# Expert choice with held weight columns, and a state-space entry normalised by feature columns

## The reference, cut to what matters

```python
# first layer, second half (x: 256 x 2048)
moe = _hier_moe(x, w_rg, b_rg, w_re, b_re, w_gate, w_up, w_down)   # logits: x @ (2048 x 36) + bias
ple = sigmoid(x @ w_pg) * (p @ w_ple)
x   = _layer_norm(ALPHA * x + moe + ple, ln2_w, ln2_b)   # (x - mean) * rsqrt(var + 1e-5) * w + b
# even layer, its entry
h = x * rsqrt(mean(x * x) + 1e-6) * norm_even_g_2        # root-mean-square norm
u, q, k, v, z = split(h @ w_in_even_2)
# state space: per state, decay magnitude exp(lr*dt) and angle li*dt; x_t = lambda x_(t-1) + B u_t; y = C x + D u
x = x + concat(attention, gated state space) @ w_out_even_2
```

## Time and profile before

| | |
|---|---|
| three runs | 3125.07, 3126.21, 3127.43 us; median 3126.21 |
| profiled execution, its own time | 3128.54 us, of which the span is 3126.8 us |
| busy share of the span | TensorE 94%, VectorE 50%, ScalarE 27%, GpSimd 7% |
| chain that ended last | TensorE 62%, VectorE 19%, DMA 12%, ScalarE 4%, issue 1%, GpSimd 1% |
| expert choice, experts | about 985 to 1081 us, 1081 to 2042 us |
| entry of the even layer, its state space loop | 2042 to 2131 us, 2131 to 2346 us |
| the rest of the even layer, the odd layer | to 2660 us, to the end |

### The profile page before, as it was taken

How to read it: one execution, slowest core, us unless ns; L and a number is a source line. 1 busy time by engine, 2 the same in 40 slices (tenths; PEclk the granted TensorE clock), 3 DMA queues, 4 the chain that set the end, 5 groups by cost and what they waited for, 6 DMA issues and landing times.

```text
span 3126.8 us, 42398 instructions
## 1 busy us (share of the span) xinstructions
PE 2943.7 (94%) x18154; PEld 2098.8 (67%) x18154; DVE 1552.9 (50%) x1879; ACT 837.6 (27%) x926; POOL 231.1 (7%) x239
## 2 busy tenths in 40 slices
PE   8999999999999999999999999879999998999898
PEld 6778777999887733333333333267758888998886
DVE  5675544574556513223222222257997554444755
ACT  4532223444433311011011110110001333444443
POOL 2001110000000000000000000035540000100100
PEclk9999998999998999999999999989999999999999
DMA  7653321455564699999999999844444465888553
GB/s 239 192 166 91 94 77 60 130 169 177 189 222 147 223 414 425 425 425 425 425 425 425 425 425 426 361 150 129 138 131 128 135 179 124 201 190 184 128 169 135
DMA packets 218362, 728.66 MB, mean 233 GB/s; under 512 B 16755, under 2 KB 19489, under 8 KB 167863
## 3 DMA queue, kind: packets, MB, share of 16 engines
q1 hardware_dynamic: 212935, 705.65, 64.4%
q0 software_dynamic: 4144, 18.14, 1.7%
q10 hardware_dynamic: 1088, 2.10, 0.2%
HBM read 720.28 MB, written 2.11 MB: 231 GB/s over the span
## 4 chain that ended last, share of the span: by engine, by line
PE 62%; DVE 19%; DMA 12%; ACT 4%; issue 1%; POOL 1%; DVEq 0%; SPq 0%; ACTq 0%
PE psum L137 60%; DVE t L287 13%; DMA t<-in_w_up 12%; ACT t L258 3%; DVE t L298 2%; DVE t L306 1%; POOL t L332 1%; PE psum L143 1%; DVE t L273 1%; ACT t L260 1%; DVE t L302 1%; DMA t<-t 0%; DVE t L310 0%; ACT L258 0%; ACT L260 0%
## 5 line engine op out<-in xcount | busy, mean ns | idle before, releaser
L137 PE MATMUL psum<-t,t 128*128 128x256 f32 (+10 forms) x17124 | 2857.9, 378 | 130.6 <-DVE t L287 77.7
L137 PEld LDWEIGHTS psum<-t,t 128*128 128x128 f32 (+6 forms) x17124 | 2016.2, 174 | 932.8 <-issue 555.4
L287 DVE TENSOR_TENSOR t<-t,t 128x1024 fp32r<-128x1024 f32 (+6 forms) x686 | 822.2, 1199 | 494.8 <-ACT t L258 449.3
L258 ACT ACTIVATE t<-t 128x1024 fp32r<-128x1024 f32 (+7 forms) x523 | 530.7, 1015 | 861.8 <-PE psum L137 572.6
L287 DVE TENSOR_TENSOR t<-t,psum 128x1024 f32<-128x1024 f32 (+3 forms) x258 | 238.2, 923 | 742.4 <-PE psum L137 446.0
L258 ACT ACTIVATE t<-psum 128x1024 f32<-128x1024 f32 (+4 forms) x278 | 213.8, 769 | 1385.4 <-PE psum L137 1280.7
L332 POOL TENSOR_TENSOR t<-t,t 128x1024 f32<-128x1024 f32 (+8 forms) x117 | 174.9, 1495 | 569.4 <-DVE t L287 423.0
L287 DVE TENSOR_TENSOR t<-psum,t 128x1024 f32<-128x1024 f32 (+6 forms) x117 | 101.1, 864 | 116.3 <-PE psum L137 85.9
L143 PE MATMUL psum<-t,t 128*128 128x128 f32 (+1 forms) x518 | 81.2, 292 | 32.0 <-DVE t L298 18.2
L143 PEld LDWEIGHTS psum<-t,t 128*128 128x128 f32 (+1 forms) x518 | 60.2, 147 | 71.2 <-issue 40.9
L83 POOL DMA_DIRECT2D t<-in_s_lr x1 | 0.6, 574 | 1185.0 <-DVE t L310 1185.0
(11 more groups left out here) (66 smaller groups left out, 219.8 us busy)
## 6 DMA issues: line engine op xcount, KB each, us to landing
t<-in_w_gate SPq DMA_DIRECT2D x128, 1024.0 KB, 16.9
t<-in_w_up SPq DMA_DIRECT2D x128, 1024.0 KB, 18.4
t<-in_w_down SPq DMA_DIRECT2D x128, 1024.0 KB, 17.4
t<-in_w_in SPq DMA_DIRECT2D x160, 512.0 KB, 3.6
t<-in_w_in_odd SPq DMA_DIRECT2D x128, 512.0 KB, 5.6
t<-in_w_in_even SPq DMA_DIRECT2D x96, 512.0 KB, 3.8
t<-in_w_out SPq DMA_DIRECT2D x32, 512.0 KB, 4.6
t<-in_w_pg SPq DMA_DIRECT2D x32, 512.0 KB, 4.6
```

The lines of the kernel that those rows point to most:

```text
L137: ins = self.e.matmul(o, l, r, start=start, stop=stop, skip_group_check=True)
L258: self.put(self.e.activation(o, i, f, scale=scale), event)
L287: self.put(self.e.tensor_tensor(o, a, b, op), event)
```

## The change

It has two parts, and some that follow from them.

**Expert choice.** `logits_of` keeps the 36 routing columns as weights and moves all 256 tokens past them: 48 matmuls give 36 x 256 logits. ScalarE copies them out of PSUM, and `route` turns them back with two matmuls against the identity, behind the second piece of `pl.g1`. The copies and subtractions for `xm` are cut in four and put in front of the four quarters of the gate projection.

The diff, cut to its core:

```diff
+def logits_of(of):
+    ps = pe.take("mo.logits", of=of)
+    pe.wait_ge(("mo.wr",))
+    for k in range(16):
+        pe.mm(ps[0:36, 0:256], wrh[:, k, :], x1T[0][:, k, :], k == 0, False)
+        pe.mm(ps[0:36, 0:256], wrh[:, k, :], x1T[1][:, k, :], False, False)
+        pe.mm(ps[0:36, 0:256], wrl[:, k, :], x1T[0][:, k, :], False, k == 15,
+              event=("mo.logits",) if k == 15 else None)
 def route(of):
     ps = pe.take("mo.route", of=of)
-    pe.wait_ge(("mo.wr",), ("landed.route",))
+    pe.wait_ge(("mo.turned",), ("landed.route",))
     for b in range(2):
         o = ps[:, 512 * b:512 * b + 36]
-        tb = slice(128 * b, 128 * b + 128)
         pe.mm(o, ones[0:1, 0:128], br[0:1, :], True, False)
-        for k in range(16):
-            pe.mm(o, x1T[0][:, k, tb], wrh[:, k, :], False, False)
-            pe.mm(o, x1T[1][:, k, tb], wrh[:, k, :], False, False)
-            pe.mm(o, x1T[0][:, k, tb], wrl[:, k, :], False, k == 15,
-                  event=("mo.route",) if b == 1 and k == 15 else None)
+        pe.mm(o, turned_logits[0:36, 128 * b:128 * b + 128], ident[0:36, 0:36], False, True,
+              event=("mo.route",) if b else None)
...
 def even():
     first = native_b("ev.u", hTe, "w_in_even_2", 3072, 1024, (1, 2))
-    for k in range(8):
-        pe.wait_ge(("ev.hT", 2 * k + 1))
-        some(first, 1)
+    def turned_pairs(j):
+        w = pe.take("ev.T", j, of=(0, 3)).rearrange("p (k b t) -> p k b t", b=2, k=4)
+        pe.wait_ge(("l2.x", j), j > 1 and ("ev.hTs", j - 2) or None)
...
+    turned_pairs(0)
+    for j in range(4):
+        if j < 3:
+            turned_pairs(j + 1)
+        for i in (2 * j, 2 * j + 1):
+            pe.wait_ge(("ev.hT", 2 * i + 1))
+            some(first, 1)
+    ps = pe.take("r1.sum", of=(0, 3))
+    pe.wait_ge(("r1.squares",), ("ev.hTs", 3))
+    pe.mm(ps[:, 0:256], ones[:, 0:128], squares[0][:, 0, :], True, True, event=("r1.sum",))
     some(first, 8)
-    rest = chain(native_b("ev.q", hTe, "w_in_even_2", 0, 1024, (0, 1)),
+    def queries():
+        work = native_b("ev.q", hTe, "w_in_even_2", 0, 1024, (0, 1))
+        for i in range(16):
+            if i < 8:
+                pe.wait_ge(("ev.hTn", i // 2))
+            yield next(work)
+    rest = chain(queries(),
                  native_b("ev.k", hTe, "w_in_even_2", 1024, 1024, (0, 1)),
                  native_a("ev.v", hTe, "w_in_even_2", 2048, 1024, (0, 1)),
...
+logits_of(other)
...
-    some(gates, 4)
+    gates = pieces_a(pe, f"pl.g{c}", x1T, 16, "w_pg", 512 * c, 512, of=other if c == 2 else first_of)
+    some(gates, 2)
+    if c == 1:
+        route(other)
+    some(gates, 2)
     if c == 2:
         rank()
     if c == 3:
...
-total = pe.take("r1.sum", of=(0,))
-for j in range(5):
-    if j < 4:
-        turn_columns("ev.T", x, j, ("l2.x", j), of=(1, 2, 3))
-    if j:
-        pe.wait_ge(("r1.square", j - 1))
-        for k in range(4):
...
+    v.wait_ge(("l2.std",))
     v.rcp(inv, stdev)
-    for ci in range(4):
-        cs = slice(512 * ci, 512 * ci + 512)
+    def centred(j):
         for b in range(2):
-            xc = x[:, b, cs]
-            v.stt(xc, xc, mv[:, b, 0:1], l2w[:, cs], ALU.subtract, ALU.mult)
-            v.stt(xc, xc, inv[:, b:b + 1], l2b[:, cs], ALU.mult, ALU.add, event=("l2.x", ci) if b else None)
...
+    def gained(j):
+        ps = v.bank("ev.T", j).rearrange("p (k b t) -> p k b t", b=2, k=4)
+        v.wait_ge(("ev.T", j))
+        for k in range(4):
+            i = 4 * j + k
+            if k == 2:
+                v.wait_ge(("r1.square", j, 1))
+            v.ts(hTe[:, i, :].rearrange("p (b t) -> p b t", b=2), ps[:, k], l2g[:, 0, i:i + 1],
+                 l2g[:, 1, i:i + 1], ALU.mult, ALU.add, event=("ev.hT", i))
+        v.names(("ev.hTs", j))
+    centred(0)
...
+    def squared(j):
+        v.wait_ge(("r1.square", 0, 0), ("r1.square", j, 0))
+        v.tt(squares[0], squares[0], squares[j], ALU.add)
...
+    gained(0)
+    centred(2)
+    gained(1)
+    centred(3)
+    gained(2)
+    squared(1)
+    gained(3)
+    squared(2)
+    squared(3)
+    s0 = squares[0]
+    v.tt(s0[:, 0:2], s0[:, 0:2], s0[:, 2:4], ALU.add)
+    v.tt(s0[:, 0], s0[:, 0], s0[:, 1], ALU.add, event=("r1.squares",))
...
+def states_in(ci):
+    v.wait_ge(("ev.u", ci))
+    v.tt(uT[:, 4 * ci:4 * ci + 4, :], v.bank("ev.u", ci).rearrange("p (m t) -> p m t", m=4), over_tokens(4),
+         ALU.mult, event=("ev.u.c", ci))
+    v.free("ev.u", ci)
+def scaled_tokens(g4):
+    v.wait_ge(("used", "s", stream.turn + 9 + 2 * g4))
+    h4 = hTe[:, 4 * g4:4 * g4 + 4, :]
+    v.tt(h4, h4, over_tokens(4), ALU.mult, event=("ev.hTn", g4))
...
+    v.split_to(first + 13)
+def low_part(c):
+    v.wait_ge(("mo.xmh", c))
+    v.tt(token_part(xm[1], c), token_part(x, c, True), token_part(xm[0], c).bitcast(F32), ALU.subtract,
+         event=("mo.xm", c))
...
     for ex in range(34):
...
+        if 8 <= ex < 11:
+            (s5_decay, s5_angles, s5_factors)[ex - 8]()
         if ex < 32:
             weighted(ex)
         if ex > 1:
...
 def even():
     s5_setup()
+    token_scales()
+    states_in(0)
+    for g4 in range(4):
+        scaled_tokens(g4)
+    states_in(1)
...
     softmax_norm("ev", 2, scs[0], mxs[0])
     softmax_norm("ev", 3, scs[1], mxs[1])
     v.limit = 1 << 20
-    v.wait_ge(("s5.phases", 7))
+    v.wait_ge(("l2.rest", 1))
...
+def s5_decay():
     v.wait_ge(("s5.dt",))
...
+def s5_factors():
     v.wait_ge(("s5.cos",))
...
+    v.tt(ci_, tA, den, ALU.mult, event=("s5.factors",))
+def s5_setup():
+    v.wait_ge(("landed.s5",))
...
-    xp = x.rearrange("p b (q j) -> p b j q", j=16)
-    for b in range(2):
-        a.copy(xm[0][:, b, :].rearrange("p (j q) -> p j q", j=16), xp[:, b], event=("mo.xmh", b))
-        a.split_to(first + 11 + 3 * b)
+    ps = a.bank("mo.logits")
+    a.split_to(first + 11)
+    a.wait_ge(("mo.logits",))
+    a.copy(turned_logits[0:36, :], ps[0:36, 0:256], event=("mo.turned",))
+    a.free("mo.logits")
...
         gathered(0, kq)
     a.wait_ge(("pl.mul", 3))
     for ex in range(33):
+        if ex == 8:
+            a.wait_ge(("landed.s5a",))
+            a.activation(dt, ld, ACT.Exp, event=("s5.dt",))
+        elif ex == 9:
+            a.wait_ge(("s5.lrdt",))
+            a.activation(mag, mag, ACT.Exp, event=("s5.mag",))
+        elif ex == 10:
+            a.wait_ge(("s5.angles",))
+            a.activation(sn, sn, ACT.Sin)
...
-    a.wait_ge(("ev.scored", 3), ("s5.phases", 7))
+    a.wait_ge(("ev.scored", 3), ("l2.rest", 1))
...
+    a.copy(token_part(xm[0], c), token_part(x, c, True), event=("mo.xmh", c))
...
-    ps = a.bank("ev.T", j).rearrange("p (b k t) -> p b k t", b=2, k=4)
...
+    a.wait_ge(("ev.T", j))
+    for k in (2, 3, 0, 1):
+        i = 4 * j + k
+        if k == 0:
+            a.wait_ge(("ev.hT", i + 1))
+        a.activation(squares[j][:, k, :].rearrange("p (b t) -> p b t", b=2), ps[:, k], ACT.Square,
+                     bias=l2c[:, 1, i:i + 1], scale=l2c[:, 0, i:i + 1], event=("r1.square", j, k // 2))
     a.free("ev.T", j)
...
-g.wait_ge(("mo.flagged",))
+g.wait_ge(("mo.flagged",), ("pl.mul", 3))
+g.load(("landed.s5a",), [(lr, I["s5_lr"]), (li, I["s5_li"]),
...
-g.wait_ge(("s5.setup",))
+g.wait_ge(("s5.factors",))
...
+g.wait_ge(("s5.setup",))
 make_phases(0)
 make_phases(1)
 for j in range(6):
     make_phases(j + 2, ("s5.phased", j))
+g.wait_ge(("s5.phases", 7))
+for h in range(2):
+    ch = slice(1024 * h, 1024 * h + 1024)
+    g.load(("landed.l2", h), [(l2w, along("ln2_w")[:, ch]), (l2b, along("ln2_b")[:, ch])])
+    g.wait_ge(("landed.l2", h))
+    for b in range(2):
+        g.tt(x[:, b, ch], x[:, b, ch], l2w, ALU.mult)
+        g.tt(x[:, b, ch], x[:, b, ch], l2b, ALU.add, event=("l2.rest", h) if b else None)
+    g.wait_ge(("l2.rest", h))
...
     quarter(i)
+s.wait_ge(("mo.gu", 27))
+pieces(stream, stream.turn, stream.turn + 4)
+s.wait_ge(("mo.gu", 31))
+pieces(stream, stream.turn + 4, stream.turn + 6)
```

More of the change, by code:

```diff
@@ L166, in __init__ @@
         self.raw, self.hi, self.lo = bufs
+        self.raw = [self.raw[(k - turn) % len(self.raw)] for k in range(len(self.raw))]
         self.known = known
@@ L498, in build @@
         gu = alloc(512)
-        xg = [alloc(4096).rearrange("p (j s) -> p j s", j=16) for _ in range(2)]
         assert top[0] == 12288
@@ L506, in build @@
         place = {key: i for i, key in enumerate(loads)}
-        loads += [("ln2_w", 0, 0), ("ln2_b", 0, 0)]
-        l2w, l2b = [slots[(len(loads) - 2 + k) % 10] for k in range(2)]
         top[0] = free_from
@@ L541, in build @@
         scratch = at(bre_at, 1024)
+        early, b2 = phases[0][0].rearrange("p i t -> p (i t)"), phases[1][0].rearrange("p a t -> p (a t)")[:, 0:512]
+        b2 = b2.rearrange("p (i c) -> p i c", i=32)
         bw = at(8192, 4096).rearrange("p (h x) -> p h x", h=16)
+        l2w, l2b = [at(6144 + 1024 * k, 1024) for k in range(2)]
         top[0] = s5_at
@@ L1336, in tensor_program @@
                     some(gates, 1)
```

(16 more changed lines are left out.)

123 lines of the change are left out of this document (63 added, 60 removed).

## The result

The changed kernel takes 3105.74 us (median of four runs, 3103.11 to 3108.61) against 3126.82 of the kernel before: a ratio of 0.9933, 95% interval 0.9916 to 0.9951. Another five runs, beside nine of the kernel before, gave 3106.54 against 3131.14: 0.9921 (0.9908 to 0.9935). It is faster by 21 to 25 us. The forecast was 3100 us, 26 us faster. They lie some 4 us further apart than the medians, since 3103.11 is the lowest of its four runs and 3128.54 lies above the median of before.

The account below looks back on a forecast made before the run. TensorE bounds the kernel, except where it waits or runs at half clock, and the weight stream in the experts. -10.0 - 15.7 - 6.4 + 6.0 = -26.1 from 3128.54: 3102.4 profiled, 3100.1 as median; range 3090 to 3112.

Parts of the forecast that it names:

- Term 1: Expert choice: 48 matmuls of 256 columns replace 96 that move 36, mostly at half clock; -10.0 us, bounds -12 and -2.5.
- The step that the stream's start carries it to the end: Experts: the gain in the choice reaches the end if the weight stream starts earlier by as much; -10.0 us.
- (b): Expert choice: the clock falls under the new 36-row matmuls too, leaving -2.5 us, so 3107.6 us; chance 0.06.
- (c): Experts: the weight stream does not start earlier, as slots are bound by landing; choice gain lost, 3110 us; chance 0.09.
- Term 2: Even entry: VectorE's first operation to the loop's first pass takes 69.4 us against 85.1; -15.7 us, bounds -17 and -12.
- Term 3: State space loop's first pass: with phases(1) made before, VectorE's copies and additions shorten; -6.4 us, between 0 and -6.4.
- Term 4: GpSimd's l2.rest beside the last passes slows VectorE's operations with SBUF operands; +6.0 us, between 0 and 9.
- the common rate of 0.34: Beside GpSimd, VectorE's operations with SBUF operands run at 0.34 of their rate; those reading PSUM at full rate.
- A half thus costs VectorE up to 6.5 us: Last passes: each half of l2.rest costs VectorE up to 6.5 us; 4.7 counted for the first, 1.3 for the rest.
- a first half that TensorE waits out in full: Sign of being wrong, last passes: TensorE waits for the whole first half of l2.rest, put at 9.85 us on GpSimd.
- Rival (a): l2.rest: each of GpSimd's eight operations costs VectorE its full 2.46 us; 14.6 us in place of 6.0, 3108.7; chance 0.12.
- Rival (d): Experts 8 to 10: setup holds ScalarE before the gates and the stream runs dry; 38 us lost, 3138 us; chance 0.05.

Follow-up runs that it names:

- late_powers: Changed kernel, but GpSimd's powers wait for the whole setup, not its early part, as before the change: 3123.61 us, 0.9979 of the kernel before.
- rest_out: Changed kernel with GpSimd's eight additions and multiplications of l2.rest left out: 3096.38 us, 0.9888 of the kernel before.
- rest_small: Changed kernel with GpSimd's eight l2.rest operations cut into 32 of 128x256 at the same place: 3102.67 us, 0.9909 of the kernel before.
- small_tables: Changed kernel with l2.rest waiting for the state space's last pass and GpSimd's table operations cut in four: 3088.99 us, 0.9879 of the kernel before.

## Why the prediction was right, step by step

**Term 1** (-10.0) measured -11.2. The logits run at full clock, 5.5 us for the 46 of 48 matmuls that the trace holds, where 6.5 were put; the tail of 1.5 us went with them, and ScalarE's copies cost at most 1.2, less than the 1.5 put on them: TensorE's waits in the choice are 0.91 and 0.65 us, where there was 0.35. The step that the stream's start carries it to the end held to 0.1 us. Rivals (b) and (c) fell: no half clock in the logits, and the stream moved.

**Term 2** (-15.7) measured -16.8. Step by step: u starts 5.15 us after VectorE's first operation, for 5.1; u, with the transposes and the sum among its slices, takes 58.3 to the transposes at 2097.54, for 59.9, as its first 32 matmuls lose 0.8 us to the clock (7.91 for 7.07) and not 2.0; and 4.9 follow to the first pass, for 4.4. late_powers showed the part that the prediction took as given, that GpSimd is not late. It had one us to spare: its two tables ended at 2101.5, the pass began at 2102.46. By the clock of the kernel before (11.6 us more) the tables ended at 2113.1, behind the 2100 to 2112 that were estimated. That it still came first was close.

**Term 3** (-6.4) measured -5.8 in the pass, at whose end VectorE now waits 0.70 us for TensorE, and some 5 in the trace where it was undone.

**Term 4** (+6.0) is the mis-sized one. It cost 8.0 us in TensorE's wait, 10.1 between two pass starts, of which 1.6 came back, and 8.8 us in the trace of rest_out. The step that failed is the common rate of 0.34: "A half thus costs VectorE up to 6.5 us", of which 4.7 were put on the path. That rate was taken from additions of 1.24 us and copies together; in the seventh pass the half met six short operations, and their rate was 1.58 / 9.61 = 0.16. One of the prediction's signs of being wrong, a first half that TensorE waits out in full, came near: 8.0 of 9.75 us. What holds is a lock per instruction, which rest_small and small_tables showed by cutting GpSimd's operations alone. This is what the Trainium skill says on the page "SBUF — State Buffer", section "SBUF: two separate sides": an exclusive lock held for the whole instruction, not a share of the bandwidth. The trace agrees, 2.25 us for 0.29 beside operations of 2.44. Rival (a), which took that rule, still gave the wrong sum of 14.6, because it counted all eight operations: the second half met 5.00 us of work that reads PSUM, which the lock leaves alone, and its 2.5 us lay beside TensorE's own work. The loads were also slower than put: GpSimd's first operation came 8.5 us behind the last table, not 4.0. The row of 4.0 us is for one load, and a half waits for two, of which the second landed 7.5 us after its issue. So the half met the six short operations, and not the scans before them; what it would have cost beside scans is not shown.

Rival (d) did not come: no wait of the experts' stream for the setup, and the time from the first expert to the entry is the same to 0.1 us.

That the sum came so near, 3102.4 for a profiled execution that took 3103.1, is in part luck. The terms were off by -1.2, -1.1, +0.6 and +2.5 us, and these errors nearly cancel; and the two profiled executions lie 25.4 us apart, where the medians lie 21.1 and 24.6 apart. The rest of the distance between 3100 and the medians is of the size of the spread of the runs, 5.5 us among four of one kernel.

Two sums beside the forecast do not come out. The lower bound of term 1, with 13 in place of 6.5, the tail of 1.5 kept and 0.7 paid once more, is -1.3 and not -2.5, so rival (b) would be 3108.8. And rivals (a) and (b) together give 3116 by the prediction's own prices, not 3113. The forecast of 3100 uses neither; the upper end of its range, 3112, leans on the second.
